# One core, a hybrid attention block: a gate slab rounded later, top-k steps earlier, sparse heads normalised ahead of the next logits

## What is computed

```python
h = rmsnorm(x);  proj = h @ w_in            # q,k,v of two branches, indexer, two gates of width 1024
# branch A, stick-breaking attention, 8 heads of 64
z = q @ k.T / 8;  attn = exp(log_sigmoid(z) + later sums of log_sigmoid(-z)), strictly causal
# branch B, sparse attention, 8 heads, 2 key heads
score = sum_h w_h * relu(q_idx_h @ k_idx.T);  idx = top_k(score, 128)
s = q @ k.T / 8 - slope * dist, only over idx;  p = softmax(s);  o = p @ v
y = (sigmoid(g_sb) * (o_sb @ W_sb) + sigmoid(g_sa) * (o_sa @ W_sa)) @ W_out;  x = x + y
x = x + relu(rmsnorm(x) @ W1)**2 @ W2
```

## Time and profile before

| | |
|---|---|
| time, median of 3 runs | 756.17 us (755.95 to 756.57) |
| the profiled execution's own time | 755.86 us |
| its span, first to last instruction | 753.8 us |
| PE busy | 732.8 us, 97% |
| PEld, DVE, ACT, POOL busy | 579.3, 525.5, 334.5, 223.6 us |
| granted TensorE clock, mean | 1.00 of full speed (2.4 GHz) |

### The profile page before, as it was taken

The page is one execution under the profiler, slowest core; times in us unless marked ns, Lnnn a source line. Parts: engine busy times, 40 slices in busy tenths (PEclk is TensorE's granted clock), DMA queues, the critical chain, the costliest instruction groups (busy, mean ns, idle before and its releaser), DMA issues.

```text
span 753.8 us, 9741 instructions
## 1 busy us (share of the span) xinstructions
PE 732.8 (97%) x3482; PEld 579.3 (77%) x3482; DVE 525.5 (70%) x730; ACT 334.5 (44%) x477; POOL 223.6 (30%) x193
## 2 busy tenths in 40 slices
PE   8999999989999999999999999999999999999998
PEld 4768778767777655678887888888888888888886
DVE  5354786698996866646664558787787969595972
ACT  5234644156664666852242344443525253524320
POOL 2113424200001455102121036362708081625610
PEclk9999999999999999999999999999999999999999
DMA  9307423310111212113163133324060514131102
GB/s 328 127 15 193 143 64 105 113 57 1 57 57 57 57 56 57 57 57 113 56 229 134 57 112 110 114 71 153 8 214 0 171 52 167 56 111 56 56 15 98
DMA packets 43893, 70.63 MB, mean 94 GB/s; under 512 B 2641, under 2 KB 27217, under 8 KB 43858
## 3 DMA queue, kind: packets, MB, share of 16 engines
q1 hardware_dynamic: 43858, 70.17, 28.4%
HBM read 65.71 MB, written 2.10 MB: 90 GB/s over the span
## 4 chain that ended last, share of the span: by engine, by line
PE 85%; DVE 7%; ACT 3%; POOL 2%; issue 1%; DMA 0%; DVEq 0%; SPq 0%; ACTq 0%; POOLq 0%
PE ps L1713 7%; PE ps L1711 7%; PE ps L1712 7%; PE ps L415 6%; PE ps L417 6%; PE ps L416 6%; PE ps L1739 6%; PE ps L1741 6%; PE ps L1740 6%; PE ps L408 5%; PE ps L410 4%; PE ps L409 4%; PE ps L1549 2%; DVE cut_lo L399 2%; PE ps L1593 1%
## 5 line engine op out<-in xcount | busy, mean ns | idle before, releaser
L1711 PE MATMUL ps<-b_hi,cut_hi 128*128 128x512 f32 (+1 forms) x272 | 102.6, 377 | 0.0
L1712 PE MATMUL ps<-b_lo,cut_hi 128*128 128x512 f32 (+1 forms) x272 | 102.4, 377 | 0.0
L1713 PE MATMUL ps<-b_hi,cut_lo 128*128 128x512 f32 (+1 forms) x272 | 102.4, 376 | 0.0
L415 PE MATMUL ps<-cut_hi,a_hi 128*128 128x512 f32 x224 | 90.0, 402 | 0.9 <-DVE a_lo L996 0.9
L417 PE MATMUL ps<-cut_hi,a_lo 128*128 128x512 f32 x224 | 87.6, 391 | 0.0
L416 PE MATMUL ps<-cut_lo,a_hi 128*128 128x512 f32 x224 | 87.4, 390 | 0.0
L399 DVE TENSOR_TENSOR cut_lo<-raw,cut_hi 128x2048 fp32r<-128x2048 f32 (+1 forms) x30 | 58.5, 1950 | 33.5 <-ACT cut_hi L391 33.5
L615 POOL TENSOR_TENSOR a_lo<-qo_sb,a_hi 128x512 fp32r<-128x512 f32 x49 | 78.2, 1629 | 5.6 <-ACT a_hi L874 5.6
L864 ACT ACTIVATE qo_sb<-ps 128x512 f32<-128x512 f32 x32 | 19.1, 598 | 136.4 <-PE ps L1713 91.8
L603 POOL TENSOR_SCALAR qo_sb<-qo_sb 128x128 f32<-128x128 f32 (+3 forms) x28 | 30.2, 1078 | 129.5 <-DVE snmax L1168 128.7
L391 ACT ACTIVATE cut_hi<-raw 128x2048 fp32r<-128x2048 f32 (+1 forms) x30 | 48.7, 1622 | 44.3 <-PE ps L410 22.7
(11 more groups left out here) (192 smaller groups left out, 1653.5 us busy)
## 6 DMA issues: line engine op xcount, KB each, us to landing
raw<-in_w_ff_dram SPq DMA_DIRECT2D x32, 1024.0 KB, 5.5
raw<-in_w_in_dram SPq DMA_DIRECT2D x16, 1024.0 KB, 5.3
gates<-in_x_dram SPq DMA_DIRECT2D x8, 512.0 KB, 7.2
raw<-in_w_out_dram SPq DMA_DIRECT2D x4, 1024.0 KB, 5.1
raw<-in_w_in_dram SPq DMA_DIRECT2D x4, 512.0 KB, 7.4
raw<-in_w_branch_sb_dram SPq DMA_DIRECT2D x2, 1024.0 KB, 5.0
raw<-in_w_branch_sa_dram SPq DMA_DIRECT2D x4, 512.0 KB, 6.1
out_dram<-gates SPq DMA_DIRECT2D x8, 256.0 KB, 2.0
```

Of the source, the lines that this page charges most:

```text
L415: nc.tensor.matmul(dst, l_hi, w_hi, start=start, stop=False)
L1711: T.matmul(dst, w_hi[:, w], b_hi[:, k, a:b], start=(k == 0), stop=False)
L1712: T.matmul(dst, w_hi[:, w], b_lo[:, k, a:b], start=False, stop=False)
L1713: mm = T.matmul(dst, w_lo[:, w], b_hi[:, k, a:b], start=False, stop=(k == KD - 1))
```

## The change

The slab that is cut second for the gates (number 11) moves. On ACT its cut stood ahead of the first `decay`; now it stands behind the second `log_of_decay`, and `gate_out(0)` behind it. On DVE its low cut stood ahead of the loop; now it is the first thing behind the second `softplus_cut`. The top-k steps between the v copies go from 1, 1, 1, 1 and one ahead of the loop to 1, 1, 5, 0 and none. In the sparse loop DVE scales head n-2 ahead of `sa_logits(n)` instead of behind it, and ACT's `gate_out` comes one head later.

```diff
@@ ScalarE, projections
-                act_cut(2 * g + 3)
+                if g < VSB:
+                    act_cut(2 * g + 3)
@@ ScalarE, stick-breaking loop
                 decay(2 * c + 1)
-                gate_out(2 * c)
+                if c:
+                    gate_out(2 * c)
                 log_of_decay(2 * c + 1)
+                if c == 0:
+                    act_cut(SL_GATE + 1)
+                    gate_out(0)
@@ ScalarE, sparse loop
-                    if q % 4 == 3 and q < 31:
-                        gate_out(8 + q // 4)
+                    if q % 4 == 0 and q:
+                        gate_out(7 + q // 4)
@@ VectorE, v projection
-                        topk(1)
-                dve_cut(2 * g + 3)
+                        topk((1, 1, 5, 0)[m])
+                if g < VSB:
+                    dve_cut(2 * g + 3)
@@ VectorE, stick-breaking loop
-            topk(1)
             for c in range(SBH // 2):
...
                 softplus_cut(2 * c + 1)
+                dve_cut(SL_GATE + 1 + c)
                 if c:
-                    dve_cut(SL_GATE + 1 + c)
                     pair_out(c - 1)
@@ VectorE, sparse loop
-                if n < 32:
-                    sa_logits(n)
                 q = n - 2
                 w, j = (q // 8 + 1) * P, q % 4
                 dve.wait_ge(p_done, q + 1)
                 link(V.reciprocal(rcp_l[:, j:j + 1], sum_p[:, j:j + 1]))
                 V.tensor_scalar(sa_s[j][:, 0:w], sa_s[j][:, 0:w], rcp_l[:, j:j + 1], None, ALU.mult).then_inc(pn_done, 1)
+                if n < 32:
+                    sa_logits(n)
```

## The result

The changed kernel takes 745.59 us (median of 4 runs, 745.44 to 745.65), the kernel before in the same session 756.06 us (755.78 to 756.57). The ratio is 0.9861, with a 95% interval of 0.9849 to 0.9873: 10.5 us faster, where 9.0 were forecast and the range ended at 746.3. The direction and the places were right; the time lies 0.7 us outside the range.

What follows compares the result with a forecast made beforehand. PE, busy for 97% of the span, was taken to bound the kernel. 3.9 us at the first sums plus 5.1 in the sparse loop made 9.0 off the median 756.17: 747.2 us, range 746.3 to 750.3 (8 in 10).

Steps and rivals of the forecast that it cites:

- What bounds the kernel: Whole kernel: PE is busy 97% of the span, so only time that PE loses can be won.
- A wait shown as x therefore delays PE by x + 0.16: PE's waits at first sums and sparse turns: lateness read from starts, 9.4 us against 7.0 by the idle column.
- The first sums: First two sums over later keys: their 4.00 us of lateness goes, fourth sum about 0.1 late, so 3.9 us won.
- the 5.44: Sparse loop: total lateness in us, by starts, of the heads' turns waiting for DVE's scaling.
- The sparse loop, taken off: Sparse loop: 5.44 less 0.10 left at heads 13 and 21 and 0.20 for late scores, 5.1 us won.
- From the span to the time: Whole kernel: 9.0 us taken off the median 756.17, since the profiled execution, 755.86, lay 0.31 under it.
- Gate exponential: ACT in the sparse loop: gate_out one head later finds its gate done, so 0.29 us of lateness at head 21 goes.
- The scaling beside POOL: DVE in the sparse loop: scaling first behind a half cut finds POOL idle and takes about 0.4 us less.
- (1): Rival: sparse loop pays only in part, 1.5 to 3.5 us come back; 6.5 us won, 749.7 us; chance 0.26.
- (2): Rival: only the first part pays, sparse turns wait as before at other heads; 752.3 us; chance 0.08.
- (4): Rival: change does nothing, PE's waits move to the third and fourth sums and other turns; 756 us; chance 0.03.
- (3): Rival: slower, scaling, logits, Exp and ACT's copy form a ring that delays PE's turn two heads on; 757.7 us; chance 0.05.

## Why the prediction was wrong

Point by point, by its own steps:

- **What bounds the kernel.** Right. Only what PE lost could be won. The experiments moved the time by what the starts of PE said, but for up to 0.8 us of the lower clock behind the wait for the first sum.
- **"A wait shown as x therefore delays PE by x + 0.16."** This is the step that failed, as a size. It is what the start of the turn is delayed by, not what PE loses. With the tail of 0.05 to 0.08 at each turn whose first weight load is not ahead, 0.88 us in the sparse loop were left out of the 5.44 (0.81 at the 14 late turns, 0.07 at head 4), and out of the upper bound of 5.4 too. It is the largest part of why the range ended too early. At the first two sums the like was there: 0.34 to the second matmul before, 0.23 and 0.25 in time.
- **The first sums.** 4.0 for 3.9. First Abs forecast at 148.3, measured 148.25; softplus 152.2 and 152.13; cast 160.96 and 160.90; third softplus 175.5 and 175.37; lateness of the fourth sum 0.1, measured 0.16. Two tails add 0.2 to the 4.00 (the third sum starts 4.28 earlier), and the fourth sum takes 0.16 and a tail of 0.09 back.
- **The sparse loop, taken off.** 0.10 for heads 13 and 21 and 0.20 for scores behind the scaling were set against the gain. Measured: 0.07 at head 21, nothing at head 13, and no wait of the scores. This is the second, smaller term: 0.2 too careful.
- **Together**: 9.0, plus 0.9 for tails in the loop, plus 0.2 for these, plus 0.1 in the first half are 10.2. The last turn starts 10.31 earlier, of which 0.06 lie ahead of the first sum, and nothing more is won behind it: the two profiled executions, both at full clock, took 755.86 and 745.54 us, 10.32 less.
- **From the span to the time.** The sum was set against the median, 756.17, which lay 0.31 above the profiled execution; in the changed kernel the two differ by 0.05. That is the other 0.3 of the 1.6 us between 747.2 and 745.59. The likely reason is the lower clock that most later executions of the kernel before show; for the three of that median it is not on record. With the sum set against the profiled execution the range would still have ended above the result.
- **Gate exponential.** In the sparse loop it waits nowhere now, as forecast. The 0.29 at head 21 was right in kind; its worth as a part of the whole is 0.9, at heads 12, 13 and 21.
- **The scaling beside POOL.** Right: behind a half cut it takes 0.42 where it took 0.80, as the next rows show.
- **Rivals.** (1), (2) and (4) needed PE waits that are not there, (3) a wait of a turn for ACT's copy, of which there is none.

DVE and then POOL at heads 19 to 23 in the changed kernel:

```profile
279.36 1.41 DVE L399 TENSOR_TENSOR cut_lo<-raw,cut_hi 128x1024 fp32r<-128x1024 f32 x1 [0.37 <-ACT cut_hi L391]
...
280.87 0.42 DVE L1202 TENSOR_SCALAR lg<-lg,rcp_l 128x384 f32<-128x384 f32 x1
281.20 0.55 DVE L1174 CUSTOM_DVE_ANT_0 lg<-ps,qo_sb 128x384 f32<-128x384 f32 x1
...
281.68 1.22 DVE L399 TENSOR_TENSOR cut_lo<-raw,cut_hi 128x1024 fp32r<-128x1024 f32 x1
```

```profile
279.07 1.49 POOL L603 TENSOR_SCALAR qo_sb<-qo_sb 128x512 f32<-128x512 f32 x1 [0.78 <-DVE snmax L1174]
281.85 2.40 POOL L603 TENSOR_SCALAR qo_sb<-qo_sb 128x512 f32<-128x512 f32 x1 [1.28 <-DVE snmax L1174]
```

The second half cut starts 0.17 us ahead of the bias and takes 1.22, the mean that the earlier trace rows has; the bias takes 2.40 instead of 1.49. The Trainium skill, in GPSIMD Engine Reference, section 1. Specifications, has GpSimd and VectorE contend for SBUF when a DVE instruction reads two SBUF inputs. The prediction held that the low cut does not bear this out. It does, and who pays depends on who starts first. In the kernel before, no half cut of the loop started ahead of a bias, and those beside one started 0.40 us or more behind it and kept their 1.22, so the earlier trace rows could not show it. In the changed kernel three start ahead, and each of their biases takes 0.91 us more (1.76, 2.08 and 2.40 for 0.85, 1.17 and 1.49). The one half cut that pays, 1.41 at 279.36, began 0.29 behind the bias of 279.07, and it lies over the 1.3 that the prediction had named as a sign of being wrong. No other engine waits for those biases, so the time did not show them. The trace of the kernel before had a subtraction of the same shape that pays in full, in the feed-forward part, 0.10 us behind one of GpSimd:

```profile
495.66 2.30 DVE L1261 TENSOR_TENSOR cut_lo<-qT_sa,cut_hi 128x1024 fp32r<-128x1024 f32 x1
495.56 1.31 POOL L615 TENSOR_TENSOR a_lo<-qo_sb,a_hi 128x512 fp32r<-128x512 f32 x1
```

## What to carry to other kernels

Count what an in-order engine loses at a wait from the starts of the instructions on both sides of it, not from the idle column; here the idle column showed 7.0 us, the late starts 9.4, and the trace of the changed kernel gave back 10.3, since a group of transposes whose weights come late is also slower itself. Compare two kernels at the same granted clock before you give a rest of some tenths of a microsecond a cause. When two engines work on one buffer in turn, move both of their parts: ACT's cut moved alone cost 4.8 us, and with DVE's part and the top-k steps it won 5.0. An edit that is worth nothing alone (the gate exponential, 0.0 us) can be worth 0.9 behind another, so try it again when the wait ahead of it has gone.

## What the runs showed of the hardware

- A group of transposes whose first weight load starts with its matmul takes 0.05 to 0.08 us longer, from its start to the next instruction, than one whose load starts 0.06 us ahead or more: 0.160 to 0.169 us to the second transpose instead of 0.108 to 0.110, in 287 of the 288 turns counted, late or not; the one other ran at the lower clock. The load was not moved by itself.
- A scaling of 384 float32 per partition takes 0.42 us with GpSimd idle and 0.80 when it starts just behind a GpSimd instruction of 1.49, which keeps its time. A subtraction of 1024 float32 with two SBUF inputs that starts 0.17 us ahead of that instruction keeps its 1.22 us and stretches it to 2.40; one that starts 0.10 us behind a GpSimd subtraction of 1.31 takes 2.30.
- Behind a wait of TensorE of 3.0 us the granted clock was 1.2 GHz for the next three microseconds in one trace and 2.4 GHz in another of kernels with the same list up to there; most executions with that wait show a mean clock of 0.995 to 0.998, all of the changed kernel 0.999 or 1.00.
